# Turning the order of 512- and 256-column products inside a weight unit of a two-layer float32 network

## What is computed

```python
def peer_ffn(x, w_q, subkeys, u, v):
    ...
        q = (xc @ w_q).reshape(PEER_CHUNK, PEER_HEADS, 2, half)
    ...
        u_e = jnp.take(u, idx, axis=0)
        v_e = jnp.take(v, idx, axis=0)
        act = jax.nn.gelu(jnp.einsum('ted,td->te', u_e, xc).astype(jnp.float32))
        return jnp.einsum('te,ted->td', (gate * act).astype(v_e.dtype), v_e)
```

## Time and profile before

| | |
|---|---|
| runs | 2355.14, 2356.43, 2358.28 us; median 2356.43 |
| profiled execution | 2356.36 us, its span 2354.5 us |
| TensorE products (PE) | 2322.8 us busy, 12380 products |
| TensorE weight loads (PEld) | 1977.7 us |
| VectorE (DVE) | 1708.0 us |
| ScalarE (ACT) | 1322.9 us |
| GpSimd (POOL) | 448.3 us |
| DMA | 408.53 MB, mean 174 GB/s |

### The profile page before, as it was taken

The page is one execution under the profiler, slowest core; times in us unless marked ns, Lnnn a source line. Parts: engine busy times, 40 slices in busy tenths (PEclk is TensorE's granted clock), DMA queues, the critical chain, the costliest instruction groups (busy, mean ns, idle before and its releaser), DMA issues.

```text
span 2354.5 us, 33293 instructions
## 1 busy us (share of the span) xinstructions
PE 2322.8 (99%) x12380; PEld 1977.7 (84%) x12380; DVE 1708.0 (73%) x3088; ACT 1322.9 (56%) x2179; POOL 448.3 (19%) x348
## 2 busy tenths in 40 slices
PE   8999999999999999999899999999999999999999
PEld 8778888899988888877688888998888888877887
DVE  7466588888975555667748898898555665777885
ACT  3454555577664544545555557766454554666554
POOL 1000233177720000000014225774000000000000
PEclk9999999999999999999999999999999999999999
DMA  7455555544456666653345555444656666433555
GB/s 254 147 179 179 162 187 188 190 143 134 135 180 195 201 193 196 218 167 126 135 151 187 191 179 162 134 135 145 213 197 204 219 200 200 137 117 124 173 189 176
DMA packets 112096, 408.53 MB, mean 174 GB/s; under 512 B 12592, under 2 KB 12640, under 8 KB 111680
## 3 DMA queue, kind: packets, MB, share of 16 engines
q1 hardware_dynamic: 107712, 391.63, 50.9%
q0 software_dynamic: 3504, 13.47, 1.7%
q10 hardware_dynamic: 720, 1.31, 0.2%
HBM read 405.30 MB, written 1.05 MB: 173 GB/s over the span
## 4 chain that ended last, share of the span: by engine, by line
PE 87%; DVE 7%; ACT 3%; DMA 2%; issue 1%; ACTq 0%; DVEq 0%
PE ps L623 23%; PE ps L626 12%; PE ps L697 11%; PE ps L701 11%; PE ps L693 10%; PE ps L875 5%; PE ps L662 3%; PE ps L659 3%; PE ps L666 3%; DVE lo L1910 2%; DMA raw<-in_peer_v 1%; PE ps L752 1%; ACT hi L1332 1%; PE ps L609 1%; PE ps L612 1%; PE ps L606 1%
## 5 line engine op out<-in xcount | busy, mean ns | idle before, releaser
L1910 DVE TENSOR_TENSOR lo<-raw,hi 128x1024 fp32r<-128x1024 f32 (+1 forms) x627 | 767.7, 1228 | 386.5 <-ACT hi L1332 382.6
L1332 ACT ACTIVATE hi<-raw 128x1024 fp32r<-128x1024 f32 x677 | 714.5, 1057 | 510.8 <-PE ps L701 264.7
L623 PE MATMUL ps<-xs,hi 128*128 128x512 f32 x2560 | 651.1, 396 | 1.1 <-ACT hi L1332 1.1
L623 PEld LDWEIGHTS ps<-xs,hi 128*128 128x128 f32 x2560 | 459.6, 189 | 83.7 <-DVE big L2832 1.3
L626 PEld LDWEIGHTS ps<-xs,lo 128*128 128x128 f32 x2560 | 349.0, 190 | 26.1
L626 PE MATMUL ps<-xs,lo 128*128 128x256 f32 x2560 | 356.7, 282 | 0.0
L2909 POOL TENSOR_SCALAR lnp<-iota,selT 128x128 f32<-128x128 f32 x256 | 300.2, 1182 | 191.3 <-PE ps L875 102.4
L693 PE MATMUL ps<-hi,lefts 128*128 128x512 f32 x986 | 304.1, 390 | 1.7 <-ACT lefts L1369 1.7
L697 PE MATMUL ps<-hi,lefts 128*128 128x512 f32 x986 | 304.0, 390 | 0.9 <-DVE lefts L1976 0.9
L701 PE MATMUL ps<-lo,lefts 128*128 128x512 f32 x986 | 303.8, 389 | 0.0
L697 PEld LDWEIGHTS ps<-hi,lefts 128*128 128x128 f32 x986 | 184.8, 188 | 40.5 <-DVE lefts L1976 2.4
(11 more groups left out here) (373 smaller groups left out, 2546.1 us busy)
## 6 DMA issues: line engine op xcount, KB each, us to landing
raw<-in_peer_u SPq DMA_DIRECT2D x256, 512.0 KB, 3.3
raw<-in_peer_v SPq DMA_DIRECT2D x256, 512.0 KB, 4.2
raw<-in_ret_vg SPq DMA_DIRECT2D x32, 512.0 KB, 3.3
raw<-in_peer_q SPq DMA_DIRECT2D x24, 512.0 KB, 3.4
raw<-in_ffn_up SPq DMA_DIRECT2D x22, 512.0 KB, 3.3
raw<-in_ffn_down SPq DMA_DIRECT2D x22, 512.0 KB, 4.3
raw<-in_ffn_gate SPq DMA_DIRECT2D x18, 512.0 KB, 4.3
raw<-in_ret_qk SPq DMA_DIRECT2D x16, 512.0 KB, 4.5
```

What stands on the lines that cost most here:

```text
L623: e.matmul(out, uh[:, k, :], xs[:, k, :, :].rearrange("p h t -> p (h t)"), start=k == 0, stop=False)
L1332: e.activation(parts(i)[0][:, 0:w], raw[:, i % N_RAW, 0:w], ACT.Copy).then_inc(s_hi, 1)
L1910: e.tensor_tensor(ul[:, 0:w], raw[:, i % N_RAW, 0:w], uh[:, 0:w].bitcast(F32), ALU.subtract).then_inc(s_lo, 1)
```

## The change

In `feat_wide` the loop of eight 512-column products and the loop of eight 256-column products become one loop. The wait for the low part stands behind the first 512-column product instead of behind the eighth.

```diff
                     xs_there(0, gen, 1, k)
                     xs_there(1, gen, 1, k)
                     e.matmul(out, uh[:, k, :], xs[:, k, :, :].rearrange("p h t -> p (h t)"), start=k == 0, stop=False)
-                e.wait_ge(*low(n))
-                for k in range(8):
+                    if k == 0:
+                        e.wait_ge(*low(n))
                     ins = e.matmul(out[:, 0:S], ul[:, k, :], xh[:, k, :], start=False, stop=k == 7)
                 ins.then_inc(s_used, 1)
```

## The result

| | before | after |
|---|---|---|
| median of nine runs each | 2356.51 us | 2363.23 us |
| lowest and highest | 2355.14, 2359.13 | 2361.17, 2364.99 |
| span of the profiled execution | 2354.5 us | 2360.1 us |

The change makes the kernel slower, by a little that is clear of the noise: the ratio is 1.0026, 95% interval 1.0017 to 1.0035, 6.7 us in the medians and 5.5 in the two profiled executions. The prediction had 2354 (range 2337 to 2370) and held "within 0.2%" for the likeliest.

What follows compares the result with a forecast made beforehand. TensorE was taken to bound the kernel, by its products' start-to-start spacing. Spacing -6 us and late low parts +2.2 and +1.8 us summed to -2, from 2356.4 to 2354 us, range 2337 to 2370.

Steps and rivals of the forecast that it cites:

- The wait, +4 us: Low weights wanted behind the first 512-column product: late low parts cost +2.2 us in the expert layers, +1.8 in the last stage.
- the query unit: In each expert layer, the unit starting at 228.27 has its low part late by 0.24 us, costing 0.18.
- the one in the middle: One unit in the middle of each expert layer has its low part late by 0.21 us, costing 0.15.
- the three at the top-k: Three units in a row while VectorE ends the top-k, late by up to 0.84 us, cost 0.78 once per layer.
- Nothing gives that back: All later TensorE products stand behind the wait and bound the time, so the +2.2 and +1.8 us remain.
- The last stage: Late low parts there, chiefly at units 2196.17 (1.44 us) and 2201.84 (0.05), cost +1.8 us; 2189.20's delay is absorbed.
- The spacing, -6 us: TensorE's products in turn take 346.7 ns a pair, 19 ns less per unit, over 320 units.
- Two readings of rows meet there: Pair spacing from changes of width (233 and 113, 346 ns) and from long runs (346.7) agree, so 346.7 was taken.
- my high end: Upper bound on spacing: wide products stay at 232 to 233 ns, no narrow one short; 353 a pair, +10 us.
- Wide products never settle: Rival: each 512-column product takes 233 ns after a 256-column one at 120; +10 us, 2370 with waits; chance 0.2.
- Short narrow ones: Rival: single 256-column products take 113 ns between 512-column ones at 226.7; 340 a pair, -23 us, 2337; chance 0.25.
- The forecast: The likeliest case: every pair of products at 346.7 ns, with waits of 4 us; chance 0.4.

Runs made afterwards that it cites:

- Pairs: The changed kernel with two 512-column and two 256-column products in turn, wait ahead of the first 256-column one; 2357.38 us, 0.9999 of the kernel before.
- fours: The changed kernel with four 512-column and four 256-column products in turn, wait ahead of the first 256-column one; 2359.79 us, 1.0011 of the kernel before.

## Why the prediction was wrong

**What bounds the kernel**: right. TensorE, at a granted clock of 1.00, before and after; only the spacing and the wait moved.

**The wait, +4 us**: the size is right by terms that offset each other, and one step is wrong. With the wait alone, the query unit is 0.20 us longer (0.18 predicted), the one in the middle 0.15 (0.15), the three at the top-k 0.77 (0.78). But "Nothing gives that back" does not hold at the top-k: right behind it TensorE had been waiting for the same VectorE work, and 0.66 of the 0.77 come back, so the three cost 0.1 us a layer. The last stage costs 3.2 less 0.7 at the hi part that it had waited for: 2.5 against 1.8. There the unit of 2196.17 paid 1.35 (1.44), and that of 2189.20 paid 0.70, taken up by the hi part as predicted. (The terms listed for that stage add up to 2.1, or 1.6 without the fifth unit.) Two later gate units, whose low parts before were on time by 0.02 us, paid 0.9 of it, and I had them at nothing. In the kernel of the change the ten units pay 4.2: 0.12 at each query unit, nothing at the one in the middle, 0.41 for the three at each top-k (in the long pattern TensorE came later to them), and 3.15 in the last stage, 0.8 of it at the two later gate units. Against this stand the 2.2 that come back, so that some 2 us are left. How much of the 0.6 at the transposes the wait gave back, and how much the spacing, cannot be told apart there. That the wait costs is shown by the kernel that has it alone.

**The spacing, -6 us**: this is the step that failed. "Two readings of rows meet there, so I take 346.7: 2774 against 2793 ns, 19 less. Times 320 units". The 2774 exists: query units and others take 2773. What was wrong is that there is one spacing for all 320. Most quiet units of `u` took 353.3 ns a pair, my high end, so the term was +2.8 us in place of -6; it accounts for the miss, since the waits came out 2 us below their term. The meeting of the two readings was chance: in the short pattern the two products take 230 and 117 ns, or 232 and 114.5 on the mean, which is neither 226.7 and 120 nor 233 and 113. I had treated the 19 ns of the old unit as a charge for a change of width that is either paid or not. Pairs at 2787 and fours at 2807 show that no such charge exists: the sum depends on the whole sequence.

**The rivals.** "Wide products never settle", 353 a pair, was right for the quiet units of `u` in its sum, and by luck: it had 233 and 120 ns, and the long pattern has 236 and 117.3 on the mean. Its argument against itself (four instructions at a looser pace) did not save the spacing. "Short narrow ones", 340, never occurred; where a narrow one took 112 to 114 in the patterns, the wide one after it took 232 or 233. The caution that a short start-to-start time is paid back by the next was right. The forecast and "Wide products never settle" stood as alternatives, and the kernel did both, by stretch.

The Trainium skill ("TensorE: Matmul & The Clock Gate", Back-to-back issue gap) gives a product N/2.4 + 2.5 ns, but calls this the gap of isolated products; for a stream of weight loads and products it names a sustained 131 ns at 512 columns. The prediction used the first for such a stream. The long runs here show neither: 226.7 ns at 512 columns. Neither figure has a term for the order of widths, and the five orders here take between 2773 and 2831 ns for the same products; the measurement decides.

**What would have shown it**: the criterion set down, a departure of the quiet unit by over 0.02 us from 2.77, was met by 2.83. The idle time before the low weights' loads came as announced, 4.7 us for "some 4", though at ten units and not at six or seven.

## What to carry to other kernels

Where an engine is full, the same instructions in another order can take another time: here up to 2% in a unit, 0.3% in the whole. Neither the spacing in long runs nor that at a single change predicted the mixed sequence: price it at both ends and run the orders that are cheap to write. Look at more than one stretch afterwards, since the same code may settle in two patterns. Moving a wait ahead costs what the late producers are late by, less what a wait behind it on the same producer would have cost anyway; look for that wait too. The few units with a late producer can keep the old place.

## What the runs showed that I had not expected

- Two stable spacings of the same instruction sequence on TensorE, 346.7 and 353.3 ns per 512- and 256-column pair, each kept over dozens of units, with the granted clock at 1.00 in both.
- 512- and 384-column products in turn take 413.3 ns a pair, 13.3 over the estimate of columns / 2.4 GHz plus 13.3 each.
- Groups of two are better than groups of four or eight (348.3, 350.9 and 349.1 ns a pair), so the cost is not monotonic in the number of changes.
- TensorE's lateness at a moved wait came back where it would have waited for the same engine anyway: 0.66 of 0.77 us in each expert layer.
- Each kernel has one trace, so whether the pattern differs from one execution to the next was not seen, and whether a weight load, the reading of the moving operand or something else makes the wide product late was not tried.
